# Unread products in TensorE's waits, and each stage's first product in two sweeps

## What is computed

```python
h = layer_norm(x, ln_in_g, ln_in_b)
for layer in range(DEPTH):
    proj = h @ w_in[layer]
    ...
    h = layer_norm(DN_ALPHA * h + mix, ln1_g[layer], ln1_b[layer])
    ...
    h = layer_norm(DN_ALPHA * h + f, ln2_g[layer], ln2_b[layer])

for l in range(DEPTH):
    h = rms_norm(x, norm1_g[l])
    z = h @ w_in[l]
    ...
    h2 = rms_norm(x, norm2_g[l])
    x = x + jnp.square(jax.nn.relu(h2 @ w_up[l])) @ w_down[l]
return rms_norm(x, final_norm_g)
```

## Time and profile before

| | |
|---|---|
| median of 3 runs | 2291.88 us (2289.19 to 2292.4) |
| the profiled execution | 2292.56 us, span 2291.2 us |
| TensorE busy with matmuls | 2131.0 us, 93% of the span |
| VectorE, ScalarE, GpSimd busy | 69%, 58%, 3% |
| mean granted TensorE clock | 0.966 of full speed |
| read from HBM | 503.49 MB, 220 GB/s over the span |

### The profile page before, as it was taken

One profiled execution on the slowest core, in us unless ns is written; L12 is line 12 of the kernel. 1 busy time (PEld: TensorE's weight loads), 2 busy tenths in 40 slices (PEclk: granted clock), 3 DMA queues, 4 the chain that ended last, 5 costly groups with the idle time before them and its releaser, 6 DMA issues.

```text
span 2291.2 us, 31949 instructions
## 1 busy us (share of the span) xinstructions
PE 2131.0 (93%) x13140; PEld 1899.0 (83%) x13140; DVE 1571.4 (69%) x1912; ACT 1339.5 (58%) x1637; POOL 73.5 (3%) x75
## 2 busy tenths in 40 slices
PE   6879989789999999999999599999899899998998
PEld 6779978567878788887877499999898799997986
DVE  5455555579898898889889767666554476665544
ACT  4634435447777777777777464565453464654543
POOL 3000002000000000000000000000110000000100
PEclk9979999989999999999999889999999899999999
DMA  8345554269999999999999735545455455544552
GB/s 280 111 131 184 184 163 154 74 193 354 323 361 325 358 336 336 345 324 361 323 360 353 262 120 176 168 154 166 137 188 201 154 172 178 171 138 139 184 200 86
DMA packets 386073, 511.42 MB, mean 223 GB/s; under 512 B 13057, under 2 KB 343937, under 8 KB 385921
## 3 DMA queue, kind: packets, MB, share of 16 engines
q1 hardware_dynamic: 380944, 498.64, 65.7%
q10 hardware_dynamic: 4976, 10.66, 1.3%
HBM read 503.49 MB, written 1.05 MB: 220 GB/s over the span
## 4 chain that ended last, share of the span: by engine, by line
PE 88%; DVE 6%; ACT 3%; issue 1%; POOL 1%; DMA 1%; ACTq 0%; DVEq 0%; POOLq 0%
PE bank L362 26%; PE bank L364 26%; PE bank L363 26%; PE bank L1131 1%; PE bank L1555 1%; DVE w_low L346 1%; PE bank L1173 1%; ACT w_high L335 1%; PE bank L1210 1%; DVE x_low L434 1%; DVE h L496 1%; DVE h L492 1%; DVE stats L485 1%; PE bank L586 1%; PE bank L1818 0%
## 5 line engine op out<-in xcount | busy, mean ns | idle before, releaser
L346 DVE TENSOR_TENSOR w_low<-raw,w_high 128x1024 fp32r<-128x1024 f32 x938 | 1134.1, 1229 | 476.4 <-ACT w_high L335 460.4
L335 ACT CAST w_high<-raw 128x1024 fp32r<-128x1024 f32 x938 | 971.1, 1050 | 511.3 <-PE bank L364 503.9
L362 PE MATMUL bank<-x_high,w_high 128*128 128x256 f32 x1888 | 541.2, 287 | 16.6 <-DVE x_low L434 16.6
L363 PE MATMUL bank<-x_low,w_high 128*128 128x256 f32 x1888 | 536.2, 284 | 0.0
L364 PE MATMUL bank<-x_high,w_low 128*128 128x256 f32 x1888 | 535.8, 284 | 0.0
L362 PEld LDWEIGHTS bank<-x_high,w_high 128*128 128x128 f32 x1888 | 362.2, 192 | 19.5 <-issue 19.2
L363 PEld LDWEIGHTS bank<-x_low,w_high 128*128 128x128 f32 x1888 | 362.2, 192 | 0.2
L364 PEld LDWEIGHTS bank<-x_high,w_low 128*128 128x128 f32 x1888 | 361.8, 192 | 0.0
L362 PE MATMUL bank<-w_high,moe_xs_high 128*128 128x512 f32 x704 | 291.2, 414 | 2.1 <-DVE moe_xs_low L1108 1.3
L364 PE MATMUL bank<-w_high,moe_xs_low 128*128 128x512 f32 x704 | 275.7, 392 | 0.0
L363 PE MATMUL bank<-w_low,moe_xs_high 128*128 128x512 f32 x704 | 274.9, 390 | 0.0
(11 more groups left out here) (322 smaller groups left out, 2602.8 us busy)
## 6 DMA issues: line engine op xcount, KB each, us to landing
raw<-in_moe_wg SPq DMA_DIRECT2D x176, 512.0 KB, 5.1
raw<-in_moe_wu SPq DMA_DIRECT2D x176, 512.0 KB, 6.6
raw<-in_moe_wd SPq DMA_DIRECT2D x88, 1024.0 KB, 6.7
raw<-in_w_in SPq DMA_DIRECT2D x84, 1024.0 KB, 5.3
raw<-in_w_up SPq DMA_DIRECT2D x32, 1024.0 KB, 5.4
raw<-in_w_down SPq DMA_DIRECT2D x32, 1024.0 KB, 4.9
raw<-in_w_out SPq DMA_DIRECT2D x16, 1024.0 KB, 4.9
raw<-in_ffn_wg SPq DMA_DIRECT2D x11, 1024.0 KB, 5.2
```

Source lines behind the costliest of these rows:

```text
L335: q.copy(high, raw).then_inc(st.cast, 1)
L346: q.tensor_tensor(low, raw, high.bitcast(F32), ALU.subtract).then_inc(st.low_made, 1)
L362: T.matmul(out, stationary[0], moving[0], start=start, stop=False, skip_group_check=True)
L363: T.matmul(out, stationary[0], moving[1], start=False, stop=False, skip_group_check=True)
```

## The change

Three things are added to TensorE's program; no other engine's program is changed.

`tensor_spin` makes products of two constants (the identity by identity and ones, 256 columns, float32) into a bank whose content nobody reads. `tensor_transposes` gets a bank and three counts: products before the first norm's wait, before the second norm's wait, and behind the transposes (bank 7). Routing has ten more before its wait for `routed`.

`first_product` takes the place of `product` for the first two pieces of a stage. It waits for one `x_low` and the third (or fourth) `x_high`, makes the 16 matmuls of the piece that read `x_high`, then waits with `x_ready` as before and makes the 8 that read `x_low`. The same 24 matmuls are made, in another order. In routing the first product stays as it is.

```diff
+def first_product(k, piece, half, bank):
+
+    T, out = k.nc.tensor, tile2(k.banks[bank])
+    T.wait_ge(k.sem("x_made"), 4 * k.transposed + 1)
+    T.wait_ge(k.sem("x_high_made"), 4 * k.transposed + 3 + half)
+    for j in range(2):
+        for kk in range(KT // 2):
+            i = half * (KT // 2) + kk
+            for w in piece:
+                T.matmul(out[:, j, :], w[:, kk, j * P:(j + 1) * P], k.x[0][:, i, :],
+                         start=(i == 0 and j == 0 and w is piece[0]), stop=False, skip_group_check=True)
+    T.wait_ge(*x_ready(k, half))
+    for j in range(2):
+        for kk in range(KT // 2):
+            i = half * (KT // 2) + kk
+            mm = T.matmul(out[:, j, :], piece[0][:, kk, j * P:(j + 1) * P], k.x[1][:, i, :], start=False,
+                          stop=(i == KT - 1), skip_group_check=True)
+    return mm
...
-def tensor_transposes(k, src, ready):
+def tensor_spin(k, bank, times):
+
+    for _ in range(times):
+        k.nc.tensor.matmul(k.banks[bank][:, 0:2 * P], k.shared[:, 0:P], k.shared[:, 0:2 * P], start=True, stop=True)
+
+
+def tensor_transposes(k, src, ready, bank, spins):
 
     T = k.nc.tensor
     ident = k.shared_const("ident")
     for t in range(TT):
+        tensor_spin(k, bank, spins[t])
         T.wait_ge(*ready[t])
         for g in range(2):
             for i in range(4):
                 mm = T.transpose(k.banks[2 * t + g][:, i * P:(i + 1) * P],
                                  src[:, t, (4 * g + i) * P:(4 * g + i + 1) * P], ident)
             mm.then_inc(k.sem("turned"), 1)
+    tensor_spin(k, 7, spins[TT])
...
-    tensor_transposes(k, k.h, [norm_ready(k, t) for t in range(TT)])
+    tensor_transposes(k, k.h, [norm_ready(k, t) for t in range(TT)], 3, (4, 11, 5) if layer else (0, 0, 6))
     for c, (name, j, _) in enumerate(MIXER_COLS):
         for half in range(2):
             piece = tensor_piece(k, k.weights)
-            if c == 0:
-                T.wait_ge(*x_ready(k, half))
             if c >= 3 and half == 0:
                 T.wait_ge(k.sem("projected"), 8 * layer + c - 2)
-            product(k, piece, k.x, half, c % 3, name == "v").then_inc(k.used, 1)
+            mm = product(k, piece, k.x, half, c % 3, name == "v") if c else first_product(k, piece, half, 0)
+            mm.then_inc(k.used, 1)
...
-    tensor_transposes(k, k.h, [norm_ready(k, t) for t in range(TT)])
+    tensor_transposes(k, k.h, [norm_ready(k, t) for t in range(TT)], 7, (4, 11, 5))
...
-    tensor_transposes(k, k.h, [norm_ready(k, t) for t in range(TT)])
+    tensor_transposes(k, k.h, [norm_ready(k, t) for t in range(TT)], 7, (4, 11, 4))
...
     mm.then_inc(k.sem("logits_turned"), 1)
+    tensor_spin(k, 7, 10)
     T.wait_ge(k.sem("routed"), 1)
...
-    tensor_transposes(k, a.xn, [norm_ready(k, t) for t in range(TT)])
+    tensor_transposes(k, a.xn, [norm_ready(k, t) for t in range(TT)], 3, (14 if layer else 48, 2, 5))
...
-    tensor_transposes(k, m.xn, [norm_ready(k, t) for t in range(TT)])
+    tensor_transposes(k, m.xn, [norm_ready(k, t) for t in range(TT)], 3, (8, 2, 6))
```

More of the change, by code:

```diff
@@ L876, in tensor_ffn @@
                 piece = tensor_piece(k, k.weights)
-                if j == 0 and which == 0:
-                    T.wait_ge(*x_ready(k, half))
                 if j >= 2 and half == 0:
                     T.wait_ge(k.sem("gate_out" if which == 0 else "gated"), j - 1)
-                product(k, piece, k.x, half, 2 * (j % 2) + which, False).then_inc(k.used, 1)
+                if j == 0 and which == 0:
+                    mm = first_product(k, piece, half, 0)
+                else:
+                    mm = product(k, piece, k.x, half, 2 * (j % 2) + which, False)
+                mm.then_inc(k.used, 1)
     for i in range(FT - TAIL):
@@ L1913, in tensor_columns @@
     piece = tensor_piece(k, k.weights)
-    if n == 0:
-        T.wait_ge(*x_ready(k, half))
     before = n - 4 if n < AB else AB - 2 + n - AB if n < AB + 2 else n - 2
@@ L1919, in tensor_columns @@
     tokens = n in (VH, VH + 1) or VA <= n < AB
-    product(k, piece, k.x, half, bank_of(n), tokens).then_inc(k.used, 1)
+    mm = product(k, piece, k.x, half, bank_of(n), tokens) if n else first_product(k, piece, half, 0)
+    mm.then_inc(k.used, 1)
 def tensor_branch(k, src, layer, u, ready):
@@ L2080, in tensor_mlp @@
             piece = tensor_piece(k, k.weights)
-            if j == 0:
-                T.wait_ge(*x_ready(k, half))
             if j >= 4 and half == 0:
                 T.wait_ge(k.sem("relu"), 16 * layer + j - 3)
-            product(k, piece, k.x, half, j % 4, False).then_inc(k.used, 1)
+            mm = product(k, piece, k.x, half, j % 4, False) if j else first_product(k, piece, half, 0)
+            mm.then_inc(k.used, 1)
     for i in range(NT2 - TAIL):
```

## The result

The changed kernel took 2272.49 us, the median of 4 runs (2270.68 to 2273.18), beside 2290.70 us for the kernel before: a ratio of 0.9919, 95% interval 0.9902 to 0.9936. The forecast was 2272. The medians lie 18.2 us apart. The profiled execution spans 2271.2 us for 2291.2.

The account below looks back on a forecast made before the run. TensorE holds 88% of the chain, so its idle time and clock were what the change could touch; stage gains of 3.3 + 2.1 + 5.6 + 1.3 + 1.0 + 1.5 + 5.7 = 20.5 us took 2292.6 to 2272, range 2265 to 2283.

Parts of the forecast that it names:

- Feed-forward, mixer 1 and both MLPs: Starts of these stages: gains of 3.3 us, 2.1 us and 2.8 us for each MLP.
- earlier start + 0.45 x slow stretch: Gain per stage: how much sooner its first product starts, plus 0.45 of the length run at the low clock.
- What an unread product costs and does: In TensorE's waits: each takes 0.43 us at the high clock, about 0.85 at the low, and counts as work.
- Rival C: In the filled waits: unread products do not hold the clock and outlast waits; about +68 us, 2360; chance 0.04.
- Routing: Router matmuls save 1.6 us, rank products 1.1, the gather 3.0: sum 5.7, bounds 2.0 and 5.7.
- rival A: Clock still falls at thinly filled places (routing, attention layers): 4.7 us less gain, 2276.8; routing 2.7; chance 0.20.
- Layer 0: Attention layer 0's start: 48 unread products begin late and slow, outlasting the norm; gain 1.0 us, bounds -0.5 and 1.7.
- Layer 1: Attention layer 1's start: product 0.5 us later, clock perhaps lost in 2 idle us; gain 1.3, bounds 0.4 and 1.6.
- Mixer 0: Mixer 0's start: six unread products behind the transposes, begun at the low clock; gain 1.5 us, bounds 0.9 and 2.7.
- An earlier start moves the stage.: After each start: the whole stage moves with it, mixers' ScalarE and GpSimd chains included, so start gains reach the total.
- rival B: Start gains are given back in mixers and experts (routing): 9.3 us less gain, 2281.4 us; chance 0.08.
- The rule on transposes: In the waits: by the skill, transposes are holes between unread products where the clock may fall; same result as rival A.

Follow-up runs that it names:

- Experiment 1: The changed kernel without the two sweeps, unread products kept: 2272.59 us, ratio 0.9927 to the kernel before.
- experiment 10: The changed kernel with about half of the unread products in each wait, 40 before attention layer 0, those behind the transposes kept: 2275.88 us, ratio 0.9939.
- experiment 4: The changed kernel with 40 instead of 48 unread products before attention layer 0, nothing else: 2269.19 us, ratio 0.9914.
- experiments 8 and 9: 8: experiment 7 plus unread products in four waits of each mixer, 2256.16 us. 9: that kernel with 7 for 4 products behind routing's transposes, 2256.26 us.
- experiment 5: The changed kernel measured again with no edit: 2271.70 us.
- experiment 3: The changed kernel with each unread product replaced by 3.6 transposes of the identity: 2269.48 us, ratio 0.9912.
- experiment 2: The changed kernel with no unread products, the two sweeps kept: 2281.02 us, ratio 0.9963.
- experiment 7: The changed kernel with 40 products before layer 0, 17 for 14 before layer 1, fewer behind transposes in mixers and attention layers: 2267.61 us, ratio 0.99.

## Why the prediction was right, point by point

- **What bounds it, and what a slow stretch is worth.** Feed-forward, mixer 1 and both MLPs came out within 0.1 us of the rule "earlier start + 0.45 x slow stretch". Experiment 1 takes out the earlier start and loses about what the rule gives it (feed-forward 0.9 us for 1.0, mixer 1 0.5 for 0.4, the MLPs 1.25 for 1.35).
- **What an unread product costs and does.** 22 instructions in 4.91 us are 0.43 us a product once the last one's tail is off, as the nearest row said. They hold the clock (experiment 1; with half of them it fell at four starts, experiment 10) and raise it (layer 0, experiment 4). Rival C is gone.
- **Routing.** 5.53 us for 5.7. The clock held through the rank products in the changed kernel, so rival A did not decide there; experiments 8 and 9 show that it can be lost there, as the rival said, for 1.45 us, half of the 3.0 I gave it.
- **Layer 0: the term that was mis-sized.** The products could not begin before 3.60 us (estimate 3.4), the clock was low, and they outlasted the norm: so far the mechanism was right. But the low stretch lasted 6.8 us, not "3 to 6", and the end came at 27.2 us after the last matmul, not 25.6: -0.3 for +1.0, near the bound of -0.5. Experiment 4 removes the overrun, and the start is 1.8 us shorter.
- **Layer 1.** 1.99 for 1.3, above the upper bound of 1.6. Two deductions were too large. The product starts 13.31 us after the last matmul for 13.24, 0.1 us later where I had taken 0.5. And the 0.3 for a clock lost in 2 us of idle time was not paid: behind 1.84 us it was kept (1.73 in experiment 5), behind 2.43 us it was lost (experiment 3).
- **Mixer 0.** 1.39 for 1.5; 0.75 more in experiment 5, where the granted clock is 1.00 from 21.6 and not from 23.6.
- **"An earlier start moves the stage."** Right outside the mixers, routing and the experts included: the rests are equal within about 0.1 us, against rival B. The prediction named the mixers among the stages that simply move, and there it was wrong. Mixer 1 gave back 1.9 of its 2.2 us, and 1.4 to 2.2 us in every profile with so early a start, so rival B was right for this one stage. Mixer 0's rest fell by 2.0 us, which cancelled it; the kernel before has 10.2 us at 0.50 from 115.8 in its one profile, where the other nine with unfilled mixers have 3.4. That the two cancelled was luck.
- **The total.** 20.0 us between the spans for 20.5 is better than its parts deserve. The forecast also starts from a profiled execution of 2292.6 us, 1.9 us above the median of the kernel before that was measured beside the result; between the medians the gain is 18.2 us. So being within 0.5 us of the measured time is in part luck, while the mechanism and the sizes at six of eight starts are not.
- **The rule on transposes.** The Trainium skill ("TensorE: Matmul & The Clock Gate", Part 4) says that they do not count as TensorE being busy in the same way. Experiments 2 and 3 decide against it here: transposes alone, 9.82 us of them in 11.80 us, kept the clock at 1.00, and they alone raised it at layer 1 (experiment 2) and at layer 0 (experiment 3).

## What to carry to other kernels

Where an engine that a whole chain hangs on must wait, look at what the wait does to its next microseconds as well as at its length: here the norms' times before the transposes stayed as they were, and about 20 us behind them went (the sweeps' part included). Fill a wait to just short of its end, and where the fill starts at the low clock count it at the slow rate: in layer 0 eight products too many cost 1.8 us, and four too many behind the transposes of an attention layer 1.7 us (layer 0, experiment 7). Then look for the stretches at the low clock inside the stages too; filling four waits in each of the two mixers won 11.5 us more, over half of what the change under study had won. And compare the rests of the stages, not only their starts: a gain at a start can be lost further on, as in mixer 1.

## What was not expected of the hardware

- Transposes hold the clock at 2.4 GHz and bring it back as float32 products do (experiment 3: 9.82 us busy of 11.80 at 1.00 with nothing else running, and from 0.50 to 1.00 at 1289.0).
- Nearly the same sequence loses the clock in one kernel and keeps it in another. The rank products kept it in seven profiles (routing's start 28.2 us) and lost it in the two with filled mixers (29.7). With unread products the low stretches at layer 0 and in the mixers last 3.4 or 6.8 us: at layer 0 6.8 us in both profiles of the changed kernel and 3.4 in experiment 1, and at the second of mixer 1's three low stretches 6.8 us behind every early start and 3.4 behind the later ones. Executions of one kernel differ too: the first low stretch in mixer 0 lasts 6.8 us in one profile of the changed kernel and 3.4 in the other, and the four runs of experiment 7 have mean granted clocks of 0.989 to 0.992 and times of 2265.84 to 2269.26 us. How much belongs to the kernel and how much to the execution, these runs do not settle.
- At one place this is worth 1.5 to 2 us, about as much as the whole spread of a kernel's runs (2 to 3 us). So two kernels whose starts differ by 4 us (layer 0's apart) can have nearly equal medians, as experiment 1 and the changed kernel did.
